# Mixture-of-experts stage of a decoder trunk: experts in pairs, one list of 128 slots and one of 64, with 4 raw and 4 split weight buffers

## The reference, cut to what matters

```python
def moe_swiglu(h, w_router, w_gate, w_up, w_down):      # D = 1024, 8 experts, width 3584
    t = h.reshape(B * S, D)
    logits = (t @ w_router).astype(jnp.float32)
    top_vals, top_idx = lax.top_k(logits, TOP_K)        # TOP_K = 2
    top_w = jax.nn.softmax(top_vals, axis=-1)
    gates = jnp.sum(jax.nn.one_hot(top_idx, N_EXPERTS) * top_w[..., None], axis=1)
    for e in range(N_EXPERTS):
        out = out + swiglu(t, w_gate[e], w_up[e], w_down[e]) * gates[:, e:e + 1]
```

## Time and profile before

| | us |
|---|---|
| median of 3 runs (1485.22 to 1486.49) | 1485.24 |
| span of the profiled execution, first to last instruction | 1484.2 |
| TensorE busy | 1467.0 |
| VectorE busy | 1165.7 |
| ScalarE busy | 961.5 |
| first expert matmul starts at | 524.93 |

### The profile page before, as it was taken

The page is one execution under the profiler, slowest core; times in us unless marked ns, Lnnn a source line. Parts: engine busy times, 40 slices in busy tenths (PEclk is TensorE's granted clock), DMA queues, the critical chain, the costliest instruction groups (busy, mean ns, idle before and its releaser), DMA issues.

```text
span 1484.2 us, 19051 instructions
## 1 busy us (share of the span) xinstructions
PE 1467.0 (99%) x7003; PEld 1217.7 (82%) x7003; DVE 1165.7 (79%) x930; ACT 961.5 (65%) x830; POOL 52.6 (4%) x51
## 2 busy tenths in 40 slices
PE   9999999999999999999999999999999999999997
PEld 8888788888888778888888888888888888888886
DVE  6464455556697698888888888888888888888897
ACT  5444453444557567777777777777777777777775
POOL 1000000000000120000000000000000000000000
PEclk9999999999999999999999999999999999999999
DMA  9744445554553279999999999999999999999992
GB/s 383 298 171 170 169 159 201 196 186 155 190 207 114 86 270 376 386 377 393 371 383 398 367 386 383 376 384 396 372 387 382 376 382 383 375 382 381 423 392 107
DMA packets 65133, 455.27 MB, mean 307 GB/s; under 512 B 7200, under 2 KB 7328, under 8 KB 11712
## 3 DMA queue, kind: packets, MB, share of 16 engines
q1 hardware_dynamic: 61456, 440.76, 77.4%
q0 software_dynamic: 3488, 13.80, 2.4%
q10 hardware_dynamic: 144, 0.09, 0.0%
HBM read 446.76 MB, written 7.86 MB: 306 GB/s over the span
## 4 chain that ended last, share of the span: by engine, by line
PE 93%; DVE 3%; issue 1%; ACT 1%; DMA 0%; POOL 0%; DVEq 0%; SPq 0%; ACTq 0%
PE psum L1625 29%; PE psum L1627 28%; PE psum L1626 28%; PE psum L2010 2%; DVE w_lo L1100 1%; PE psum L1672 1%; PE psum L1673 1%; PE psum L1671 1%; PE psum L1681 1%; ACT w_hi L779 1%; PE psum L1703 0%; PE psum L1695 0%; DMA x_sb<-in_x 0%; DVE x_sb L1550 0%; DVE work L1324 0%
## 5 line engine op out<-in xcount | busy, mean ns | idle before, releaser
L1100 DVE TENSOR_TENSOR w_lo<-raw,w_hi 128x2048 fp32r<-128x2048 f32 (+1 forms) x420 | 948.8, 2274 | 233.7 <-ACT w_hi L779 232.1
L779 ACT CAST w_hi<-raw 128x2048 fp32r<-128x2048 f32 (+1 forms) x420 | 799.3, 1903 | 323.1 <-PE psum L1627 307.3
L1625 PE MATMUL psum<-w_hi,actA_hi 128*128 128x512 f32 (+1 forms) x1320 | 519.0, 393 | 3.5 <-DVE actA_lo L1458 1.8
L1627 PE MATMUL psum<-w_hi,actA_lo 128*128 128x512 f32 (+1 forms) x1320 | 511.4, 387 | 0.0
L1626 PE MATMUL psum<-w_lo,actA_hi 128*128 128x512 f32 (+1 forms) x1320 | 510.5, 387 | 0.0
L1625 PEld LDWEIGHTS psum<-w_hi,actA_hi 128*128 128x128 f32 x1320 | 248.0, 188 | 55.1 <-DVE w_lo L1100 2.6
L1627 PEld LDWEIGHTS psum<-w_hi,actA_lo 128*128 128x128 f32 x1320 | 247.8, 188 | 51.8
L1626 PEld LDWEIGHTS psum<-w_lo,actA_hi 128*128 128x128 f32 x1320 | 248.3, 188 | 47.6
L1625 PE MATMUL psum<-w_hi,actB_hi 128*128 128x512 f32 x624 | 244.7, 392 | 0.0
L1627 PE MATMUL psum<-w_hi,actB_lo 128*128 128x512 f32 x624 | 243.0, 389 | 0.0
L1626 PE MATMUL psum<-w_lo,actB_hi 128*128 128x512 f32 x624 | 242.8, 389 | 0.0
(11 more groups left out here) (197 smaller groups left out, 639.6 us busy)
## 6 DMA issues: line engine op xcount, KB each, us to landing
raw<-in_moe_w_gate SPq DMA_DIRECT2D x112, 1024.0 KB, 7.2
raw<-in_moe_w_up SPq DMA_DIRECT2D x112, 1024.0 KB, 7.2
raw<-in_moe_w_down SPq DMA_DIRECT2D x112, 1024.0 KB, 7.1
raw<-in_ret_w_in SPq DMA_DIRECT2D x22, 1024.0 KB, 12.4
raw<-in_ffn_w_gate SPq DMA_DIRECT2D x11, 1024.0 KB, 4.8
raw<-in_ffn_w_up SPq DMA_DIRECT2D x11, 1024.0 KB, 4.8
raw<-in_ffn_w_down SPq DMA_DIRECT2D x10, 1024.0 KB, 4.8
raw<-in_ret_w_out SPq DMA_DIRECT2D x8, 1024.0 KB, 4.7
```

Of the source, the lines that this page charges most:

```text
L779: nc.scalar.copy(w_hi[:, u % SPLIT_SLOTS, 0:size], raw[:, u % RAW_SLOTS, 0:size]).then_inc(sem["hi_ready"], 1)
L1100: nc.vector.tensor_tensor(w_lo[:, slot, 0:size], raw[:, u % RAW_SLOTS, 0:size], as_f32(w_hi[:, slot, 0:size]), ALU.subtract).then_inc(sem[ ...
L1625: nc.tensor.matmul(dst, l_hi[:, k, cols], r_hi[:, kk, rcols], start=first, stop=False)
L1627: return nc.tensor.matmul(dst, l_lo[:, k, cols], r_hi[:, kk, rcols], start=False, stop=last)
```

## The change

- The experts are ranked by the number of their tokens, expert 0 always first; the first four get **long lists** of 128 slots, the other four **short lists** of 64 slots. A short list's activations are stacked, 64 high and 64 low columns in one stationary tile of 128, so **two passes** do (`short_pass`), by high and by low weights; the upper and lower halves of the result are added afterwards, by a matmul with a constant (`fold`) in the hidden layer, and by ScalarE and VectorE in the output.
- A long and a short expert form a **pair**; the loop runs over pairs (3 rounds, and the last pair after it), and units of both come **in turn** (`step_units`): 12 units a step, the short one's work one step behind.
- **4 raw and 4 split buffers** for 7 and 3; AHEAD becomes 3, in all stages.
- SyncE reads expert ids from SBUF (`experts_of`) in each round, and after four expert units waits for the ranking. The ranking and the sorting of places and gates by rank are new small operations on VectorE. In one round of the loop there are two indirect fetches and two stores, of 128 and 64 rows.
- If a long list held over 128 tokens, or a short one over 64, all pairs would be gone through a second time.

The diff, cut to its core:

```diff
-LIST = 96
-PASSES = -(-SEQ // LIST)
+LONG, SHORT = P, P // 2
+EXPERT_PAIRS = N_EXPERTS // 2
+ROUNDS = SEQ // LONG
-RAW_SLOTS = 7
-SPLIT_SLOTS = 3
+RAW_SLOTS = 4
+SPLIT_SLOTS = 4
+START_SPLIT = 3
 AHEAD = SPLIT_SLOTS - 1
-ITEM_UNITS = STEPS * 6
+ITEM_UNITS = STEPS * 12
...
+            def step_units(n):
+                first = [("up", 1, n - 1), ("gate", 0, n)] if n else [("gate", 0, n)]
+                second = [("up", 0, n), ("down", 1, n - 2)] if n >= 2 else [("up", 0, n)]
+                third = [("down", 0, n - 1), ("gate", 1, n)] if n else [("gate", 1, n)]
+                return [(*one, half) for stage in (first, second, third) for half in range(2) for one in stage]
...
+            load_units(n_dense, first_units[:4], [None, None])
+            sp.wait_ge(sem["ranked"], 1)
+            short_first = sp.value_load(expert_ids[0:1, 3 * EXPERT_PAIRS:3 * EXPERT_PAIRS + 1], min_val=0, max_val=N_EXPERTS - 1)
+            load_units(n_dense + 4, first_units[4:], [None, short_first])
             sp.wait_ge(sem["routed"], 1)
-            trip = sp.value_load(trips[0:1, 0:1], min_val=N_EXPERTS - 1, max_val=PASSES * N_EXPERTS - 1)
+            trip = sp.value_load(trips[0:1, 0:1], min_val=EXPERT_PAIRS - 1, max_val=ROUNDS * EXPERT_PAIRS - 1)
             with sp.Fori(0, trip) as i:
                 w.item = i
-                for kind, ahead, s, u in item_blocks(False)[lead:]:
-                    load_block(u, kind, (i + ahead) % N_EXPERTS, s)
-                for kind, _, s, u in item_blocks(False)[:lead]:
-                    load_block(u + ITEM_UNITS, kind, (i + 1) % N_EXPERTS, s)
+                now, then, seen = experts_of(i), experts_of(i + 1), set()
+                u = first_loop_unit
+                for n in range(2, STEPS + 2):
+                    u = load_units(u, step_units(n), now, then, seen)
...
+            def expert_step(at, n, used, limit):
+                gates, ups, downs = used + (4 if n else 2), used + (8 if n >= 2 else 6 if n else 4), used + (12 if n >= 2 else 10 if n else 6)
+                if n:
+                    hi_through(min(used + 3 + AHEAD, limit))
+                    act.wait_ge(sem["pe_done"], w.pe(at, "short_up", n - 1))
+                    nc.scalar.copy(short_up, bank((at, "short_up", n - 1))).then_inc(sem["short_up"], 1)
+                hi_through(min(gates + AHEAD, limit))
+                act.wait_ge(sem["pe_done"], w.pe(at, "long_gate", n))
+                if n:
+                    act.wait_ge(sem["long_hid"], w.at("long_hid", n))
+                nc.scalar.activation(e_sil, bank((at, "long_gate", n)), ACT.Silu).then_inc(sem["long_sil"], 1)
...
+                hi_through(min(ups + AHEAD, limit))
...
+                if n:
+                    short_silu(at, n - 1)
...
+                if n:
+                    hi_through(min(ups + 2 + AHEAD, limit))
+                    short_rounded(n - 1)
...
+                hi_through(min(downs + AHEAD, limit))
+                act.wait_ge(sem["pe_done"], w.pe(at, "short_gate", n))
+                nc.scalar.copy(short_gate, bank((at, "short_gate", n))).then_inc(sem["short_gate"], 1)
+                act.wait_ge(sem["pe_done"], w.pe(at, "long_turn", n))
+                nc.scalar.copy(eT_hi, bank((at, "long_turn", n))).then_inc(sem["long_turn_hi"], 1)
+                return downs
...
+            def short_pass(dst, left, right, kk, rcols, first, last):
+                r_hi, r_lo = right
+                nc.tensor.matmul(dst, left, r_hi[:, kk, rcols], start=first, stop=False)
+                return nc.tensor.matmul(dst, left, r_lo[:, kk, rcols], start=False, stop=last)
...
+            def expert_step(at, n, units):
+                short, short_downs, following = n >= 1, n >= 2, n % STEPS == 0
+                rows = 0 if n == 0 else 2
+                if short:
+                    short_hidden((at, "short_up", n - 1), 0, units)
+                if following:
+                    pe.wait_ge(sem["long_lo"], w.at("long_lo", rows + 1))
+                long_hidden((at, "long_gate", n), 0, units)
+                if short:
+                    short_hidden((at, "short_up", n - 1), 1, units)
+                if n == STEPS:
+                    turn_short_rows(at, 0)
+                if following:
+                    pe.wait_ge(sem["long_lo"], w.at("long_lo", rows + 2))
+                long_hidden((at, "long_gate", n), 1, units)
+                if n == 0:
+                    short_gather(("short_gather",))
+                long_hidden((at, "long_up", n), 0, units)
+                if n == STEPS:
+                    turn_short_rows(at, 1)
+                if short_downs:
+                    short_down(at, n - 2, 0, units)
+                long_hidden((at, "long_up", n), 1, units)
...
+                if short_downs:
+                    short_down(at, n - 2, 1, units)
+                if short:
+                    fold(at, n - 1)
+                    long_down(at, n - 1, 0, units)
...
+                for half in range(2):
+                    if following:
+                        pe.wait_ge(sem["short_rows_lo"], w.at("short_rows_lo", rows + half + 1))
+                    short_hidden((at, "short_gate", n), half, units)
+                    if short and half == 0:
+                        long_down(at, n - 1, 1, units)
+                turn_hidden(at, n)
```

More of the change, by code:

```diff
@@ L398, in work_order @@
[L398 to L432, removed]
@@ L436, in work_order @@
+    for n in range(2):
+        expert_step("first", n)
+    o.last[G1], o.last[U1] = ("short_out", 1), ("short_out", 2)
+    start, banks = (o.n, len(o.unit_done)), list(o.last)
+    for n in range(2, STEPS + 2):
+        expert_step("pair", n)
     per_item = o.n - start[0]
@@ L440, in work_order @@
     del o.unit_done[start[1]:]
-    item("last", True)
+    for n in range(2, STEPS):
+        expert_step("last", n)
+    expert_end("last")
     o.last_units = o.unit_done[start[1]:]
+    del o.unit_done[start[1]:]
     return o, per_item
@@ L634, in load @@
                     sp.wait_ge(sem["lo_ready"], w.at("lo_ready", u - RAW_SLOTS + 1))
[L635 to L646, removed]
+                slot = u % RAW_SLOTS
@@ new lines, in load, with load_expert @@
+                sp.dma_start(raw[:, slot, 0:kk * n], src).then_inc(sem["raw_in"][slot], 16)
+            def load_expert(u, kind, expert, s, half, new):
+                v = e_w[kind][bass.ds(expert, 1)] if expert is not None else e_w[kind][0:1]
+                if new:
+                    sp.wait_ge(sem["lo_ready"], w.at("lo_ready", u - RAW_SLOTS + 1))
+                    sp.sem_inc(sem["expert_asked"], 1)
+                load(u, v[:, s, half].rearrange("o p n -> p (o n)"), *((2, D) if kind == "down" and s < STEPS - 1 else (4, BLK)), waited=new)
@@ new lines, in load_units, with experts_of @@
+            def load_units(u, units, now, then=None, seen=None):
+                for kind, which, s, half in units:
+                    block = (kind, which, s < STEPS)
+                    load_expert(u, kind, now[which] if s < STEPS else then[which], s % STEPS, half, seen is not None and block not in seen)
+                    if seen is not None:
+                        seen.add(block)
+                    u += 1
+                return u
+            def experts_of(i):
+                return [sp.value_load(expert_ids[0:1, bass.ds(i + which * 3 * EXPERT_PAIRS, 1)], min_val=0, max_val=N_EXPERTS - 1)
+                        for which in range(2)]
@@ new lines, in combine @@
+            def combine(key):
+                pe.wait_ge(sem["slots_turn"], 2)
+                for k in range(2):
+                    for q in range(4):
+                        c, t = divmod(q, 2)
+                        pe.wait_ge(sem["os_lo"], 2 * k + c + 1)
+                        dst, cols = bank((*key, q)) if k else ready((*key, q)), slice(c * BLK, (c + 1) * BLK)
+                        nc.tensor.matmul(dst, slots[:, k, tokens(t)], os_hi[k][:, cols], start=k == 0, stop=False)
+                        mm = nc.tensor.matmul(dst, slots[:, k, tokens(t)], os_lo[k][:, cols], start=False, stop=k == 1)
+                        if k:
+                            group(mm, *key, q)
```

783 lines of the change are left out of this document (492 added, 291 removed).

## The result

The changed kernel takes 1521.88 us in the median of 4 runs (1512.96 to 1528.71), against 1485.23 us for the kernel before (1485.19 to 1486.49) on the same chip: ratio 1.024, 95% interval 1.020 to 1.028. It is slower, as forecast, but by 37 us and not by 15. The profiled execution took 1519.83 us, 2.1 us more than its span.

The account below looks back on a forecast made before the run. The prediction took TensorE to bound the kernel before, and the round of four raw buffers the changed one: start 542 - 2, 327 x 2.83 cadence, 24 end, 11 other traffic and ids, 1500 us in all; range 1410 to 1535.

Parts of the forecast that it names:

- what would show it: Expert stretch: chain through loads, casts, subtractions; casts wait for loads; TensorE busy five sixths; landings 6.5 to 7.1, 370 GB/s.
- the step (L + c)/4: Expert loads: one raw buffer's round shared by four buffers gives the cadence, 2.83 us a unit; the forecast case, chance 0.50.
- L: Expert loads: landing time of a 1 MiB load from issue, taken as 6.9 us, between 4.8 and 7.1.
- c: Rest of a raw buffer's round after landing: cast 1.92, subtraction 2.29, handovers, 0.13 for waits; taken as 4.4 us.
- start: Before the paced expert loads: fifth expert unit's low part ends at 542 us, less 2 as first four buffers free quickly.
- other traffic and ids: Expert stretch: reading back, indirect fetches and stores 8 us (0 to 16), plus 3 for SyncE's expert ids: 11.
- the end: After the last load is asked for: 13 us to the last matmul, then 11 as before; 24 in the sum.
- T: Expert stretch: cadence, the time from one expert load to the next; forecast at 2.83 us a unit.
- Landings did not shorten to 5.9: Rival, expert loads: fewer loads at once land in 5.9 us, cadence 2.58, kernel 1419 us (1393 to 1481); chance 0.38.
- The rate limit: Rival, expert loads: HBM reads cannot exceed 358 GB/s, so 2.93 us a unit and 1533 us; chance 0.03.
- The clock: Rival, TensorE in the experts: idling drops it to 1.2 GHz, 57 us a pair's step, over 2100 us; chance 0.01.
- the lists fitted: Rival, expert loop: lists don't fit, a second round adds 336 units, about 2450 us; chance 0.02.

## Why the prediction was right and where it was wrong

- **The mechanism held.** The round of four raw buffers sets the pace. The chain runs through loads, subtractions and casts; casts wait for loads; two more raw buffers, shorter loads, and halved casts each give time back, and less TensorE work (within the 9 us by which the medians differ, in runs that spread over 16 to 19) and results taken off PSUM earlier do not. All that the section on what would show it asked for is in the trace, but for the busy share of TensorE: 91% of 600 to 1300, where it said five sixths. Its work is 2.5 and not 2.39 us a unit; besides, the record of a matmul is longer than the distance to the next, and stretches from 0.39 to 0.63 us where the clock is low.
- **The forecast failed in the size of the cadence**, the step (L + c)/4 with L = 6.9 and c = 4.4, and in c above all, where 0.13 us stood for waits behind other work. Measured were L = 7.05 and c = 4.59, 2.905 us a unit over the 327 loads. Sum against the span: start 542 - 2 against 538.6, -1.4; cadence 950.0 against 925.4, +24.6; other traffic and ids, booked apart at 11, are inside that cadence, -11; the end 29.1 against 24, +5.1. That is +17.3 over 1500.4, the span of 1517.7. The rest is that the median of the runs lies 4.2 us above this span and not 1.0.
- **Why c was too small.** Cast and subtraction were right to 0.01. The waits in a round are 0.12 us before the cast, 0.16 between cast and subtraction and 0.10 from there to the next load, 0.38 in all, where the prediction had 0.06 for handovers and 0.13. The work beside the casts comes bunched: at two neighbouring units of the twelve of a step the subtraction begins 0.46 us after the cast's end, at the others 0.03 to 0.25, and over the twelve units from 723 on c goes from 4.4 to 5.4. At four buffers the missing 0.19 is worth 327 x 0.19/4 = 15.5 us. Which of the copies and products makes how much of it was not tried apart.
- **L was right only with the other traffic taken out, and at a slower pace than forecast.** Of the 320 loads issued between 560 and 1500, 279 met no packet of the indirect and read-back queue, and their mean landing is 6.86 us; the other 41 took 8.36. That is 41 x 1.5/4 = 15 us, where the prediction booked 8 for traffic. But the landing goes with the pace: 5.25 at a cadence of 3.25, 7.05 at 2.91, 7.35 at 2.83, 8.65 at 2.61 (means of all loads; the kernel before, with landings of 7.2 in the mean and 7.1 in the median of 600 to 1300, ran at 2.8). At the forecast's own 2.83, L with its traffic would be 7.35, as with halved casts, and c would have had to be 4.0. L and T had to be solved together; on a line through the points at 2.91 and 2.83, an estimate, even c = 4.4 gives 2.885 us and not 2.83.
- **The other traffic** was sized rightly (6.82 MB on the indirect and read-back queue from 560 to 1500, where 6.7 were counted) but belongs in the round, since it lengthens the landings that it meets: of eleven landings over 9.0 us, ten lie in three stretches in which that queue moved 0.5 to 2.4 MB.
- **The start** was right to 3.4 us: the fifth unit's part of the round is over at 538.6 and not 542, since the ranking began 1.4 us before the 521.0 that the sum took, and the 2.6 us allowed for slower operations were not needed.
- **The end** was 5.1 us longer: the last matmuls begin 1.4 us after the last low part, because of the short product, they are 16 and not 8 (1.8 us), and 1.6 us go to the low clock.
- **The rivals.** Landings did not shorten to 5.9; 388 GB/s were held for 32 us and then lost. The rate limit falls by two versions that read 397 and 410 GB/s over 700 us. By the Trainium skill (DMA: Bandwidth & Descriptors, Where 436 GB/s comes from) some 358 GB/s would have bound them; the Trainium skill (HBM Reference, Specifications (TRN2)) says that a core that streams alone gets well above its share of the domain, some 425, and the runs agree with that. The clock fell only a little (0.97 over 600 to 1300), in short stretches at 1.2 GHz, each beside a wait of TensorE of 2.1 to 4.7 us, and the loads set the pace regardless; the lists fitted, 336 loads were made.

## What to carry to other kernels

The time of a buffer's round, landing plus all that is done before it is given back, divided by the number of buffers, is a bound on the cadence like an engine's busy time; work it out before trading buffers away. The landing in it is not a constant but rises as loads come faster, so read it at two paces and solve for both, and take its mean, not its median; in the one pair of runs that tells, half of what was taken out of the round came back as landing. Here the saving on TensorE was real: with six raw buffers to carry it the kernel gained 31 us, and with halved casts 59.

## What the runs showed of the hardware

- A third load in flight is worth little. With 3 raw buffers a load of 1 MiB lands in 4.8 us in the median, as if alone, at 329 to 339 GB/s; with 4 it takes 7.0, at 370. One buffer more, a third of the buffers, bought 9 to 12% more rate (12% in the same kernel).
- By rule, the Trainium skill (DMA: Bandwidth & Descriptors, Latency and other measured facts) has the HBM access at 0.2 us on average and 2 us at high load. By the rows the rate alone isn't the load that counts: at 339 GB/s, 92% of the 370, the median landing was that of a load by itself.
- The changed kernel's time scatters over 1.0%, with AHEAD 2 over 1.1% and with one pass over 1.2%, where the kernel before and the version with 6 raw buffers keep within 0.1 to 0.2%. That loads set the pace isn't enough for it: with halved casts the spread is 0.2%, with 3 raw buffers 0.1 and 0.2% in two runs each, though the halves ran on another chip than AHEAD 2 and the one pass. What differs between the executions stays open.
- A short idle time can be followed by the low clock: TensorE, busy from 1488.6 to 1498, stood still for 2.59 us and, 1.5 us after it had begun again, ran for 3.4 us at 1.2 GHz.
